# Gated linear attention on one core: attends and value transposes moved to other PSUM banks, and a head's gate work moved beside its own query strips

## The chip, the cores and the metric

The kernel runs on one core of one Trainium2 chip. The metric is the device time of one execution in microseconds (us). TensorE (PE) multiplies matrices into PSUM, VectorE (DVE) and ScalarE (ACT) work on what it leaves there, SyncE (SP) issues the transfers from HBM, and GpSimd (POOL) has nothing to do.

## The reference

The reference is a decoder trunk of two layers over 528 tokens of width 1024 (16 meta tokens and 512 inputs). Layer 0 is gated linear attention (GLA) with 4 heads, a key width of 256 and a value width of 512 per head. Layer 1 is an attention with forget gates (FoX) with 16 heads. What the change touches is layer 0, cut here to what matters:

```python
def gla_layer(h, norm_g, w_in, w_gate_up, b_gate, head_norm_g, w_out):
    proj = rmsnorm(h, norm_g) @ w_in
    q, k, v, g_low, r = jnp.split(proj, [o1, o2, o3, o4], axis=-1)
    log_a = jax.nn.log_sigmoid((g_low @ w_gate_up + b_gate)) / GLA_GATE_NORMALIZER
    q = q.reshape(B, L, GLA_HEADS, GLA_HEAD_K) * (GLA_HEAD_K ** -0.5)
    ...
    o = gla_chunked(q, k, v, log_a)       # S_t = diag(a_t) S_{t-1} + k_t^T v_t, o_t = q_t S_t
    o = rmsnorm(o, head_norm_g).reshape(B, L, D_INNER)
    return h + (o * jax.nn.silu(r)) @ w_out
```

## The kernel before

**Strips.** A strip is a projection of the normalised input onto 128 output columns: `strip(job, x1)` (L1146) runs 8 k-tiles, and for each k-tile three products (high by high, high by low, low by high part) over two halves of 264 tokens, 48 matmuls in all. Its weights come as one 512 KB transfer into `raw`; ACT copies them to `w_hi` (L348) and DVE makes the rest `w_lo` (L684). Both do that in `split`, and `ahead(name)` splits the chunk that lies three strips behind the named one. In `ahead` DVE waits until ACT has made the same chunk's `w_hi`. A head of GLA has 12 strips: two of queries (Q), two of keys (K), four of values (V) and four of the output gate (R).

**Jobs and slots.** PE's work is a list of named jobs. Besides the strips a head has two gate products G (`gate_logits`, L1190: the low-rank gate times its up projection), four value transposes X (`transposed`, L1179) and four attends A (`gla_attend`, L1223, the scores times a 128-column part of the values). The job of each name takes one of two slots of two PSUM banks (banks 0 and 1, or 2 and 3) by the parity of its number in the list (`slot`, L217). `wait_slot` (L254) lets PE write a slot only when the job two places earlier in the list has been read: a Q strip by `q_made`, a K strip by `k_made`, a V strip by `vt_made`, an R strip by `r_made`, a G by `g_abs` and `g_min`, an X by `vlo_made`, an A by `y_made`. The scores (`gla_scores`, L1199) lie in banks 4 to 7, and the sum of squares of the last head's output (`sum_squares`, L1168) in banks 4 and 5.

**The gate chain of a head.** When G{h}0 and G{h}1 are done, ACT takes their absolute value (L387), then the exponential (L389) and the logarithm (L391), each with its own table load, and DVE the minimum with zero (L733), the difference and the running sum `b_` (L739). Then DVE forms four differences of `b_` (`minus_at`), and ACT eleven exponentials of them (`decays`, L396, one table load). DVE multiplies queries and keys with these (`muls_q`, L758, and `muls_k`, L785), and only then can the scores of that head start.

**The order.** Every engine's order is written out by hand. In a head h PE runs: Q0, the sum of squares of head h-1, Q1, K0, K1, V0, R0, X0, V1, scores, R1, A0, X1, V2, then the gate products of head h+1, A1, X2, V3, R2, A2, X3, R3, A3. The gates and decays of head h+1 thus run on ACT and DVE during head h; those of head 0 run in front, during the first strips. `gla_value` (L422) copies a V strip into the one buffer `gvt`, from which X transposes it. `gla_out` (L845) makes `y` of an attend, after ACT has squared the attend (`gla_square`, L454). `head_norm` (L854) is a reciprocal and two multiplications of head h-1's `y`, once ACT's `root` (L360) has read the sum of squares. On DVE `gla_gate` (R strip to `gsr`) of R1 is followed by `ahead("V{h}2")` and `gla_out(h, 0)`.

After the four heads come the output projection (W0 to W7), then the 16 heads of FoX, which use the two slots by the same parity.

The lines that say which jobs exist and where they go:

```python
def slot(job):
    return 2 * (JOB[job] % 2)
...
b = JOBS[JOB[job] - 2]      # wait_slot: whose readers must be done
```

Of the kernel before, what the change touches and what calls it, by code (L numbers as in the profile page):

```python
# [11 lines left out]
P = 128  # L12
# [62 lines left out]
def gla_strips(h):  # L75
    return [f"Q{h}0", f"Q{h}1", f"K{h}0", f"K{h}1", f"V{h}0", f"R{h}0", f"V{h}1", f"R{h}1", f"V{h}2", f"V{h}3", f"R{h}2", f"R{h}3"]
# [18 lines left out]
JOB = {j: n for n, j in enumerate(JOBS)}  # L95

# [15 lines left out]
def program(nc, xT, consts, vecs, w_low, w_up, w_all, w_f, out):  # L112
    with ExitStack() as c:
# [88 lines left out]
        fkf = acc  # L202
        fsr, fvt = sq[:, 0, 0:SEQ], sq[:, 1, :]
# [13 lines left out]
        def slot(job):  # L217
            return 2 * (JOB[job] % 2)

# [34 lines left out]
        def wait_slot(pe, job):  # L254

            if JOB[job] < 2:
                return
            b = JOBS[JOB[job] - 2]
# [82 lines left out]
        def _(act):  # L341
# [39 lines left out]
            def gates(h):  # L381
                for t in range(CT):
                    done(act, f"G{h}{t}")
                    if h:
                        act.wait_ge(mul_made, (h - 1) * len(MULS) + MULS.index("qj0") + 1)
                    col = B_GATE + h * CT + t
                    nc.scalar.activation(two(s1[:, t, :]), halves(slot(f"G{h}{t}")), ACT.Abs, bias=vec[:, col:col + 1]).then_inc(g_abs, 1)  # L387
# [34 lines left out]
            def gla_value(h, v):  # L422
                done(act, f"V{h}{v}")
                if 4 * h + v:
                    before = f"X{h}{v - 1}" if v else f"X{h - 1}3"
                    done(act, before)
                nc.scalar.activation(two(gvt[:]), halves(slot(f"V{h}{v}")), ACT.Copy).then_inc(vt_made, 1)
# [46 lines left out]
            ahead("Q00")  # L474
            ahead("Q01")
            gates(0)
            ahead("K00")
            decays(0)
            for h in range(GLA_HEADS):
                if h:  # L480
# [12 lines left out]
                gla_gate(h, 0)  # L493
# [4 lines left out]
                gla_scores_hi(h)  # L498
                gla_gate(h, 1)
                ahead(f"V{h}2")  # L500
                gla_square(h, 0)
                gla_values_hi(h, 1)
                gla_value(h, 2)
                if h + 1 < GLA_HEADS:
                    gates(h + 1)
                ahead(f"V{h}3")
                gla_square(h, 1)
                gla_values_hi(h, 2)
                if h + 1 < GLA_HEADS:
                    decays(h + 1)  # L510
                gla_value(h, 3)
                ahead(f"R{h}2")
                gla_gate(h, 2)
                ahead(f"R{h}3")
                gla_square(h, 2)
                gla_values_hi(h, 3)
                gla_gate(h, 3)
                if h + 1 == GLA_HEADS:
                    y_high(0)
                gla_square(h, 3)  # L520
# [158 lines left out]
        def _(dve):  # L679
# [43 lines left out]
            dve.wait_ge(rtok_done, 1)  # L723
            nc.vector.tensor_copy(rtok[:, 0:NBLK], bank(6, 0, NBLK * 32).rearrange("p (b n) -> p b n", n=32)[:, :, 0]).then_inc(rtok_made, 1)
            nc.vector.tensor_copy(rtok[0:META, NBLK:NBLK + 1], bank(6, 128, 129, 0, META)).then_inc(rtok_made, 1)

            def gates(h):
                for t in range(CT):
                    dve.wait_ge(g_abs, 2 * h + t + 1)
                    if h:  # L730
                        dve.wait_ge(exp_made, h * len(EXPS))
                    col = B_GATE + h * CT + t
                    nc.vector.tensor_scalar(two(s2[:, t, :]), halves(slot(f"G{h}{t}")), vec[:, col:col + 1], 0.0, ALU.add, ALU.min).then_inc(g_min, 1)  # L733
# [132 lines left out]
            ahead("Q00")  # L866
            gla_query(0, 0)
            ahead("Q01")
            gla_query(0, 1)
            dve.wait_ge(cst_loaded, 16)  # L870
            gates(0)
            ahead("K00")
            decays(0)
            gla_key(0, 0)
            for h in range(GLA_HEADS):
                if h:
                    ahead(f"Q{h}0")
                    gla_query(h, 0)
                    head_norm(h - 1)
                    ahead(f"Q{h}1")  # L880
# [12 lines left out]
                ahead(f"R{h}1")  # L893
                gla_mask(h)
                gla_scores_lo(h)
                gla_gate(h, 1)
                ahead(f"V{h}2")
                gla_out(h, 0)
                gla_values_lo(h, 1)
                if h + 1 < GLA_HEADS:  # L900
                    gates(h + 1)
                ahead(f"V{h}3")
                gla_out(h, 1)
                gla_values_lo(h, 2)
                if h + 1 < GLA_HEADS:
                    decays(h + 1)
                ahead(f"R{h}2")
                gla_gate(h, 2)
                ahead(f"R{h}3")
                gla_out(h, 2)  # L910
                gla_values_lo(h, 3)
                gla_gate(h, 3)
# [212 lines left out]
        def _(pe):  # L1125
# [64 lines left out]
            def gate_logits(h):  # L1190
                for t in range(CT):
                    job = f"G{h}{t}"
                    wait_slot(pe, job)
                    c0 = h * GLA_DK + t * P
                    for n in range(2):
                        i = nc.tensor.matmul(halves(slot(job))[:, n, :], up[:, c0:c0 + P], glow[:, n * HALF:(n + 1) * HALF], start=True, stop=True)
                    i.then_inc(job_done, 1)

            def gla_scores(h):  # L1199
                pe.wait_ge(mul_made, (h + 1) * len(MULS))  # L1200
                pe.wait_ge(rstd_made, h + 1)
                if h == 0:
                    pe.wait_ge(rtok_made, 2)
# [46 lines left out]
            pe.wait_ge(rstd_made, 1)  # L1250
            rstd_by_token()
            pe.wait_ge(glow_made, 1)
            pe.wait_ge(up_loaded, 32)
            gate_logits(0)
            for h in range(GLA_HEADS):
                if h:
                    strip(f"Q{h}0", x1)
                    pe.wait_ge(hacc_made, 3 * h)
# [3 lines left out]
                for s in (f"K{h}0", f"K{h}1", f"V{h}0", f"R{h}0"):  # L1262
                    strip(s, x1)
                pe.wait_ge(vt_made, 4 * h + 1)
                transposed(f"X{h}0", gvt)
# [7 lines left out]
                if h + 1 < GLA_HEADS:  # L1273
                    gate_logits(h + 1)
                gla_attend(h, 1)
                pe.wait_ge(vt_made, 4 * h + 3)
                transposed(f"X{h}2", gvt)
                strip(f"V{h}3", x1)
                strip(f"R{h}2", x1)
                gla_attend(h, 2)  # L1280
                pe.wait_ge(vt_made, 4 * h + 4)
                transposed(f"X{h}3", gvt)
                strip(f"R{h}3", x1)
                gla_attend(h, 3)

# [195 lines left out]
```

## Time and profile before

| | us |
|---|---|
| median of 3 runs | 1192.83 (1192.6 to 1192.99) |
| the profiled execution's own time | 1195.57 |
| its span | 1193.8 |
| PE busy | 1107.8 (93%) |
| DVE busy | 612.2 (51%) |
| ACT busy | 496.3 (42%) |
| mean granted clock of PE | 0.965 of full |

The profiled execution is 2.7 us above the median, and its span leaves 1.8 us of its own time outside. PE is the engine to read: what counts is where it waits, and which chain on ACT and DVE ends the wait. The four GLA heads take the first 451 us, the output projection and FoX the rest.

### The profile page before, as it was taken

The page shows a single profiled execution, that of the slowest core. Times are in us where ns is not written, and L with a number is a line of the kernel's source. Part 1 is how long each engine was busy: PE and PEld are TensorE (multiplying, and loading weights), DVE is VectorE, ACT ScalarE, POOL GpSimd, SP SyncE. Part 2 cuts the span into 40 slices and gives each one's busy share as a digit, 9 for nine tenths or more (in the row PEclk, how much of TensorE's full clock was granted, in tenths as well). Part 3 has the DMA queues.
Part 4 walks back from the last instruction along what each step waited for, and adds up shares of the span by engine and source line. Part 5 has one row for each costly group of instructions (what it writes and reads, how often), then busy time and mean ns, then how long its engine had stood idle before and what let it go on. Part 6 is the DMA issues. An engine that isn't in the chain of part 4 may idle for free.

```text
span 1193.8 us, 18411 instructions
## 1 busy us (share of the span) xinstructions
PE 1107.8 (93%) x7716; PEld 1011.7 (85%) x7716; DVE 612.2 (51%) x1032; ACT 496.3 (42%) x869; POOL 0.2 (0%) x4
## 2 busy tenths in 40 slices
PE   6897999799799999999799999999999999998995
PEld 5786998799799899998688888888888888886883
DVE  5664473556457437535445554455455555564233
ACT  5624523723452325424434444444444444454221
POOL 0000000000000000000000000000000000000000
PEclk9898999899999999999899999999999999998997
DMA  6111121112112111222111222112211212211211
GB/s 224 53 54 36 54 89 54 42 65 89 37 54 80 63 54 57 103 89 71 54 66 59 71 71 71 57 68 72 71 57 68 71 55 70 72 56 51 92 50 70
DMA packets 23762, 81.77 MB, mean 68 GB/s; under 512 B 2784, under 2 KB 3040, under 8 KB 23680
## 3 DMA queue, kind: packets, MB, share of 16 engines
q1 hardware_dynamic: 23680, 80.59, 19.4%
q8 instruction: 61, 1.00, 0.3%
q14 instruction: 21, 0.17, 0.0%
HBM read 78.49 MB, written 2.10 MB: 68 GB/s over the span
## 4 chain that ended last, share of the span: by engine, by line
PE 83%; DVE 9%; ACT 4%; issue 3%; DMA 0%; DVEq 0%; ACTq 0%; SPq 0%
PE psum L1138 68%; PE psum L1378 3%; PE psum L1364 2%; PE psum L1207 2%; DVE w_lo L684 2%; ACT w_hi L348 1%; DVE y L691 1%; PE psum L1347 1%; PE psum L1361 1%; PE psum L1349 1%; PE psum L1350 1%; PE psum L1348 1%; DVE y L845 1%; DVE gsr L691 1%; DVE y_lo L691 1%
## 5 line engine op out<-in xcount | busy, mean ns | idle before, releaser
L684 DVE TENSOR_TENSOR w_lo<-raw,w_hi 128x1024 fp32r<-128x1024 f32 x144 | 174.9, 1220 | 81.9 <-ACT w_hi L348 81.7
L1138 PE MATMUL psum<-xh,w_hi 128*128 128x264 f32 x768 | 165.1, 297 | 35.6 <-DVE y L845 27.9
L348 ACT ACTIVATE w_hi<-raw 128x1024 fp32r<-128x1024 f32 x144 | 149.9, 1048 | 100.0 <-PE psum L1138 100.0
L1138 PE MATMUL psum<-xl,w_hi 128*128 128x264 f32 x768 | 161.0, 292 | 0.0
L1138 PE MATMUL psum<-xh,w_lo 128*128 128x264 f32 x768 | 160.0, 291 | 0.0
L1138 PEld LDWEIGHTS psum<-xh,w_hi 128*128 128x128 f32 x768 | 124.3, 197 | 40.8 <-DVE w_lo L684 29.1
L1138 PEld LDWEIGHTS psum<-xl,w_hi 128*128 128x128 f32 x768 | 124.3, 196 | 0.0
L1138 PEld LDWEIGHTS psum<-xh,w_lo 128*128 128x128 f32 x768 | 124.2, 196 | 0.0
L1138 PE MATMUL psum<-zh,w_hi 128*128 128x264 f32 x512 | 106.2, 289 | 5.9 <-DVE y L691 3.2
L1138 PE MATMUL psum<-zl,w_hi 128*128 128x264 f32 x512 | 104.4, 286 | 0.0
L1138 PE MATMUL psum<-zh,w_lo 128*128 128x264 f32 x512 | 104.1, 285 | 0.0
L1138 PE MATMUL psum<-x2h,w_hi 128*128 128x512 f32 x256 | 103.3, 404 | 0.0
L1138 PE MATMUL psum<-y_lo,w_hi 128*128 128x264 f32 (+1 forms) x384 | 102.1, 320 | 0.0
L1138 PE MATMUL psum<-x2h,w_lo 128*128 128x512 f32 x256 | 101.8, 398 | 0.0
L1138 PE MATMUL psum<-x2l,w_hi 128*128 128x512 f32 x256 | 101.0, 395 | 0.0
L1138 PEld LDWEIGHTS psum<-zh,w_hi 128*128 128x128 f32 x512 | 80.8, 190 | 10.5 <-issue 9.0
L1138 PEld LDWEIGHTS psum<-zl,w_hi 128*128 128x128 f32 x512 | 79.9, 189 | 0.0
L1138 PEld LDWEIGHTS psum<-zh,w_lo 128*128 128x128 f32 x512 | 79.7, 189 | 0.0
L1003 DVE TENSOR_REDUCE top<-psum 128x1 f32<-128x144 f32 (+1 forms) x64 | 30.8, 504 | 78.3 <-PE psum L1351 78.3
L1138 PEld LDWEIGHTS psum<-y_lo,w_hi 128*128 128x128 f32 x384 | 63.7, 188 | 5.8
L1138 PEld LDWEIGHTS psum<-x2h,w_lo 128*128 128x128 f32 x256 | 48.1, 188 | 11.3
L1138 PEld LDWEIGHTS psum<-x2l,w_hi 128*128 128x128 f32 x256 | 48.3, 188 | 10.8
(239 smaller groups left out, 1896.8 us busy)
## 6 DMA issues: line engine op xcount, KB each, us to landing
raw<-w_all SPq DMA_DIRECT2D x144, 512.0 KB, 3.2
hT<-xT SPq DMA_DIRECT2D x8, 264.0 KB, 5.4
outT<-hT SPq DMA_DIRECT2D x8, 256.0 KB, 2.3
cst<-consts SPq DMA_DIRECT2D x1, 528.0 KB, 6.9
y<-w_up_ SPq DMA_DIRECT2D x2, 64.0 KB, 8.1
low_raw<-w_low SPq DMA_DIRECT2D x1, 64.0 KB, 2.1
f_raw<-w_f SPq DMA_DIRECT2D x1, 64.0 KB, 8.2
vec<-vecs SPq DMA_DIRECT2D x1, 22.5 KB, 1.6
```

The costliest lines, as they stand in the source:

```text
L348: nc.scalar.activation(w_hi[:, n % HI_RING, :], raw[:, n % LO_RING, :], ACT.Copy).then_inc(hi_made, 1)
L684: nc.vector.tensor_tensor(w_lo[:, n % LO_RING, :], raw[:, n % LO_RING, :], w_hi[:, n % HI_RING, :].bitcast(F32), ALU.subtract).then_inc(lo ...
L691: nc.vector.tensor_tensor(out, a, b, op).then_inc(made, 1)
L845: nc.vector.scalar_tensor_tensor(y[:, n, :], joined(slot(f"A{h}{v}")), vec[:, G_HEAD + v:G_HEAD + v + 1], gsr[:, v % 2, :], op0=ALU.mult, ...
L1003: nc.vector.tensor_reduce(top[:, b:b + 1], scores(b), op=ALU.max, axis=AX.XY if b == NBLK - 1 else AX.X, negate=True).then_inc(max_made, 1)
L1138: i = nc.tensor.matmul(o, w[a][:, k % KT, :], x[b][:, k, c0:c1], start=k == first and a == b == 0, stop=k == last and a == 1)
L1207: i = nc.tensor.matmul(out, lhs[:, t], rhs[:, t], start=t == 0, stop=t == CT - 1)
L1347: nc.tensor.matmul(o, fq_hi[:, cols], fk_hi[:, k0:k1], start=True, stop=False)
L1348: nc.tensor.matmul(o, fq_hi[:, cols], fk_lo[:, k0:k1], start=False, stop=False)
L1349: nc.tensor.matmul(o, fq_lo[:, cols], fk_hi[:, k0:k1], start=False, stop=False)
L1364: i = nc.tensor.transpose(bank(bk, c0, c0 + BLK), pr[b][:, BLK * j:BLK * j + BLK], ident)
L1378: i = nc.tensor.matmul(bank(slot(job), PT_Q0[j], SEQ), vs[a][0:rows, j, :], ps[b][0:rows, AF_AT[j]:AF_AT[j] + w], start=j == 0 and a == b ...
```

## The change

- The place of a job is now a table, `PLACE`. Attends (and G01) go to banks 4 and 5, value transposes and the other gate products to banks 6 and 7, and the strips (with the jobs of the later stages) alternate on the two old slots. `wait_slot` waits for the readers of the job that was last in the same place (`BEFORE`).
- `gvt` becomes two buffers, the second of them a row of `y`.
- The gate products of head h+1 leave the middle of head h: G{h+1}0 comes at the end of head h, and G{h+1}1 behind Q{h+1}0. The absolute values, the exponential, the logarithm, the running sum and the decays of a head now run in that head, beside its Q and K strips: between `ahead` of Q0 and `ahead` of K1.
- In those parts the key strip K0 is read (`gla_key(h, 0)`) in the middle of DVE's decays, and K1 behind them and behind `ahead("K{h}1")`.
- V3 and R2 change places, each A and X comes behind the next strip, the scores follow R1, and the scores now also wait for X0's readers. `rstd_by_token` moves from ahead of head 0's gate products to between K00 and K01.

```diff
 def gla_jobs(h):
-    gate = [f"G{h + 1}0", f"G{h + 1}1"] if h + 1 < GLA_HEADS else []
-    first = ["G00", "G01"] if h == 0 else []
-    return ([f"Q{h}0", f"Q{h}1"] + first + [f"K{h}0", f"K{h}1", f"V{h}0", f"R{h}0", f"X{h}0", f"V{h}1", f"R{h}1", f"A{h}0", f"X{h}1",
-            f"V{h}2"] + gate + [f"A{h}1", f"X{h}2", f"V{h}3", f"R{h}2", f"A{h}2", f"X{h}3", f"R{h}3", f"A{h}3"])
+    first = ["Q00", "Q01", "G00", "G01"] if h == 0 else [f"Q{h}0", f"G{h}1", f"Q{h}1"]
+    return (first + [f"K{h}0", f"K{h}1", f"V{h}0", f"R{h}0", f"X{h}0", f"V{h}1", f"R{h}1", f"V{h}2", f"A{h}0", f"X{h}1", f"R{h}2",
+                     f"A{h}1", f"X{h}2", f"V{h}3", f"A{h}2", f"X{h}3", f"R{h}3", f"A{h}3"] + ([f"G{h + 1}0"] if h + 1 < GLA_HEADS else []))
...
+PLACE, BEFORE = {}, {}
+_slots = 0
+for _job in JOBS:
+    if _job[0] == "A" or _job == "G01":
+        PLACE[_job] = 4
+    elif _job[0] in "XG":
+        PLACE[_job] = 6
+    else:
+        PLACE[_job] = 2 * (_slots % 2)
+        _slots += 1
+    _same = [j for j in PLACE if PLACE[j] == PLACE[_job]]
+    BEFORE[_job] = _same[-2] if len(_same) > 1 else None
...
@@ ACT, one head (h > 0) @@
+                    gate_abs(h, 0)
                     ahead(f"Q{h}0")
+                    gate_abs(h, 1)
                     root(f"h{h - 1}", GLA_DV, T)
+                    gate_log(h)
+                    ahead(f"Q{h}1")
...
                     ahead(f"K{h}0")
+                decays(h)
                 ahead(f"K{h}1")
                 ahead(f"V{h}0")
                 gla_value(h, 0)
...
@@ DVE, one head (h > 0) @@
+                    gate_min(h, 0)
                     ahead(f"Q{h}0")
                     gla_query(h, 0)
+                    gate_min(h, 1)
+                    ahead(f"Q{h}1")
                     head_norm(h - 1)
-                    ahead(f"Q{h}1")
                     gla_query(h, 1)
-                    ahead(f"K{h}0")
-                    gla_key(h, 0)
+                gate_sums(h)
+                ahead(f"K{h}0")
+                decays(h)
                 ahead(f"K{h}1")
+                gla_key(h, 1)
                 muls_q(h)
-                gla_key(h, 1)
                 ahead(f"V{h}0")
                 muls_k(h)
                 ahead(f"R{h}0")
                 gla_gate(h, 0)
...
@@ DVE decays @@
                 minus_at(s1, 32, 15)
                 minus_at(s2, 64, 31)
+                gla_key(h, 0)
                 exped(h, "kd")
                 minus_at(s1, 128, 63)
...
@@ PE, one head @@
                 if h:
                     strip(f"Q{h}0", x1)
+                    gate_logits(h, 1)
                     pe.wait_ge(hacc_made, 3 * h)
                     pe.wait_ge(glo_made, 5 * h)
                     sum_squares(f"h{h - 1}")
                     strip(f"Q{h}1", x1)
...
                 strip(f"V{h}1", x1)
+                strip(f"R{h}1", x1)
                 gla_scores(h)
-                strip(f"R{h}1", x1)
+                strip(f"V{h}2", x1)
                 gla_attend(h, 0)
-                pe.wait_ge(vt_made, 4 * h + 2)
-                transposed(f"X{h}1", gvt)
-                strip(f"V{h}2", x1)
-                if h + 1 < GLA_HEADS:
-                    gate_logits(h + 1)
+                gla_transposed(h, 1)
+                strip(f"R{h}2", x1)
                 gla_attend(h, 1)
...
                 strip(f"R{h}3", x1)
                 gla_attend(h, 3)
+                if h + 1 < GLA_HEADS:
+                    gate_logits(h + 1, 0)
```

## Rows read from the trace of the kernel before

**Rows 1.** The page: PE's busy time and granted clock over the whole span

```profile
PE 1107.8 (93%) x7716; PEld 1011.7 (85%) x7716; DVE 612.2 (51%) x1032; ACT 496.3 (42%) x869; POOL 0.2 (0%) x4
...
PEclk9898999899999999999899999999999999998997
```

**Rows 2.** Windows by head; stretch, its length, busy times, PE clock, DMA

```profile
18.32:144.33 126.01, 109.42 (x826) 103.72 (x826) 65.57 (x99) 58.43 (x98) 0.00 (x0) 0.89 0.17 58
...
250.13:355.96 105.83, 96.62 (x813) 93.22 (x813) 56.77 (x89) 44.26 (x75) 0.00 (x0) 0.95 0.17 60
355.96:451.14 95.18, 91.23 (x804) 88.59 (x804) 47.65 (x81) 30.41 (x55) 0.00 (x0) 1.00 0.19 68
```

**Rows 3.** The chain that ended last, head 2; start, length, piece

```profile
257.04 29.21 PE psum L1138 x240
...
293.22 6.33 PE psum L1207 x125
...
316.10 1.99 PE psum L1196 x8
...
329.29 13.61 PE psum L1138 x96
...
347.34 6.08 PE psum L1138 x48
...
355.96 6.03 PE psum L1138 x48
361.98 0.89 PE psum L1170 x4
```

**Rows 4.** Waits of PE in head 2 (257 to 363 us): total, times, longest

```profile
PE psum L1138 <- DVE y L845: 8.1, 3, 5.5
```

**Rows 5.** Timeline of ACT around head 2's gate chain and the next root

```profile
318.83 1.28 ACT L389 ACT_TABLE_LOAD   x1
320.13 1.08 ACT L389 ACTIVATE s<-s 128x1056 f32<-128x1056 f32 x1
...
332.25 1.28 ACT L400 ACT_TABLE_LOAD   x1 [5.95 <-DVE s L691]
...
340.14 0.59 ACT L427 ACTIVATE gvt<-psum 128x528 f32<-128x528 f32 x1
340.63 1.05 ACT L348 ACTIVATE w_hi<-raw 128x1024 fp32r<-128x1024 f32 x1
...
362.91 0.70 ACT L360 ACTIVATE sq<-psum,eps 128x528 f32<-128x528 f32 x1 [4.06 <-PE psum L1170]
```

**Rows 6.** Timeline of DVE in the same head

```profile
257.81 3.45 DVE L696 RECIPROCAL acc<-sq 128x528 f32<-128x528 f32 x1 [0.92 <-ACT sq L360]
...
263.65 1.22 DVE L684 TENSOR_TENSOR w_lo<-raw,w_hi 128x1024 fp32r<-128x1024 f32 x1
264.79 0.70 DVE L800 SCALAR_TENSOR_TENSOR q<-psum,rstd 128x528 f32<-128x528 f32 x1
...
271.06 1.22 DVE L691 TENSOR_TENSOR qd<-qd,q 128x1024 f32<-128x1024 f32 x1
...
281.46 0.18 DVE L691 TENSOR_TENSOR km<-km,k 128x32 f32<-128x32 f32 x1
...
323.65 1.26 DVE L691 TENSOR_TENSOR s<-s 128x1056 f32<-128x1056 f32 x1 [4.03 <-ACT s L391]
324.94 2.41 DVE L739 TENSOR_TENSOR_SCAN b<-cst,s 128x528 f32<-128x528 f32 x2
...
330.97 2.34 DVE L691 TENSOR_TENSOR s<-b 128x1024 f32<-128x1024 f32 x2
```

**Rows 7.** Timeline of PE: four of the five transposes of a value strip

```profile
286.19 0.60 PE L1184 MATMUL psum<-cst,gvt 128*128 128x128 f32 x4
```

**Rows 8.** The chain that ended last, head 0 and the end of head 3

```profile
32.71 0.70 DVE y L691
...
65.52 7.62 PE psum L1138 x48
...
442.51 6.09 PE psum L1138 x48
```

More of the change, by code:

```diff
@@ L75, in gla_strips @@
 def gla_strips(h):
[L76 removed]
+    return [f"Q{h}0", f"Q{h}1", f"K{h}0", f"K{h}1", f"V{h}0", f"R{h}0", f"V{h}1", f"R{h}1", f"V{h}2", f"R{h}2", f"V{h}3", f"R{h}3"]
 def gla_jobs(h):
[L80 to L83 removed]
+    first = ["Q00", "Q01", "G00", "G01"] if h == 0 else [f"Q{h}0", f"G{h}1", f"Q{h}1"]
+    return (first + [f"K{h}0", f"K{h}1", f"V{h}0", f"R{h}0", f"X{h}0", f"V{h}1", f"R{h}1", f"V{h}2", f"A{h}0", f"X{h}1", f"R{h}2",
+                     f"A{h}1", f"X{h}2", f"V{h}3", f"A{h}2", f"X{h}3", f"R{h}3", f"A{h}3"] + ([f"G{h + 1}0"] if h + 1 < GLA_HEADS else []))
 def fox_step(h):
@@ L202, in program @@
         fkf = acc
+        gvt2 = (gvt[:], y[:, YT - 1, :])
         fsr, fvt = sq[:, 0, 0:SEQ], sq[:, 1, :]
@@ L217, in slot @@
         def slot(job):
-            return 2 * (JOB[job] % 2)
+            return PLACE[job]
         def joined(b):
@@ L254, in wait_slot @@
         def wait_slot(pe, job):
-            if JOB[job] < 2:
+            b = BEFORE[job]
+            if b is None:
                 return
-            b = JOBS[JOB[job] - 2]
             kind = b[0]
@@ L379, in _, with gate_abs, gate_log @@
             root("x", D_MODEL, T)
[L381 to L387, printed above, removed]
+            def gate_abs(h, t):
+                done(act, f"G{h}{t}")
+                if h:
+                    act.wait_ge(mul_made, (h - 1) * len(MULS) + MULS.index("qj0") + 1)
+                col = B_GATE + h * CT + t
+                nc.scalar.activation(two(s1[:, t, :]), halves(slot(f"G{h}{t}")), ACT.Abs, bias=vec[:, col:col + 1]).then_inc(g_abs, 1)
+            def gate_log(h):
                 act.wait_ge(g_abs, 2 * h + 2)
@@ L423, in gla_value @@
                 done(act, f"V{h}{v}")
[L424 to L427, printed above, removed]
+                if 4 * h + v >= 2:
+                    done(act, f"X{h}{v - 2}" if v >= 2 else f"X{h - 1}{v + 2}")
+                nc.scalar.activation(two(gvt2[v % 2]), halves(slot(f"V{h}{v}")), ACT.Copy).then_inc(vt_made, 1)
             def gla_values_hi(h, v):
@@ L472, in y_high @@
                     nc.scalar.activation(y_hi[:, i, :], y[:, i, :], ACT.Copy).then_inc(yhi_made, 1)
[L474 to L478, printed above, removed]
-            for h in range(GLA_HEADS):
-                if h:
+            for h in range(GLA_HEADS):
+                if h == 0:
+                    ahead("Q00")
+                    ahead("Q01")
+                    gate_abs(0, 0)
+                    gate_abs(0, 1)
+                    gate_log(0)
+                    ahead("K00")
+                else:
+                    gate_abs(h, 0)
                     ahead(f"Q{h}0")
+                    gate_abs(h, 1)
                     root(f"h{h - 1}", GLA_DV, T)
+                    gate_log(h)
+                    ahead(f"Q{h}1")
                     if h == 1:
@@ L492, in _ @@
                 ahead(f"R{h}0")
-                gla_gate(h, 0)
                 gla_values_hi(h, 0)
@@ L497, in _ @@
                 ahead(f"R{h}1")
-                gla_scores_hi(h)
+                gla_gate(h, 0)
                 gla_gate(h, 1)
                 ahead(f"V{h}2")
+                gla_scores_hi(h)
+                gla_value(h, 2)
                 gla_square(h, 0)
                 gla_values_hi(h, 1)
-                gla_value(h, 2)
-                if h + 1 < GLA_HEADS:
-                    gates(h + 1)
-                ahead(f"V{h}3")
+                ahead(f"R{h}2")
+                gla_gate(h, 2)
                 gla_square(h, 1)
                 gla_values_hi(h, 2)
-                if h + 1 < GLA_HEADS:
-                    decays(h + 1)
+                ahead(f"V{h}3")
                 gla_value(h, 3)
-                ahead(f"R{h}2")
-                gla_gate(h, 2)
-                ahead(f"R{h}3")
                 gla_square(h, 2)
                 gla_values_hi(h, 3)
+                ahead(f"R{h}3")
                 gla_gate(h, 3)
@@ L722, in _, with gate_min, gate_sums @@
             tt(glow, glow, rstd[0:48, :], ALU.mult, glow_made)
[L723 to L733, printed above, removed]
+            def gate_min(h, t):
+                dve.wait_ge(g_abs, 2 * h + t + 1)
+                if h:
+                    dve.wait_ge(exp_made, h * len(EXPS))
+                col = B_GATE + h * CT + t
+                nc.vector.tensor_scalar(two(s2[:, t, :]), halves(slot(f"G{h}{t}")), vec[:, col:col + 1], 0.0, ALU.add, ALU.min).then_inc(g_min, 1)
+            def gate_sums(h):
                 dve.wait_ge(g_ln, h + 1)
@@ L864, in y_low @@
                     tt(y_lo[:, i, :], y[:, i, :], y_hi[:, i, :].bitcast(F32), ALU.subtract, ylo_made)
[L866 to L874, printed above, removed]
-            for h in range(GLA_HEADS):
-                if h:
+            for h in range(GLA_HEADS):
+                if h == 0:
+                    ahead("Q00")
+                    gla_query(0, 0)
+                    ahead("Q01")
+                    gla_query(0, 1)
+                    gate_min(0, 0)
+                    gate_min(0, 1)
+                    dve.wait_ge(rtok_done, 1)
+                    nc.vector.tensor_copy(rtok[:, 0:NBLK], bank(6, 0, NBLK * 32).rearrange("p (b n) -> p b n", n=32)[:, :, 0]).then_inc(rtok_made, 1)
+                    nc.vector.tensor_copy(rtok[0:META, NBLK:NBLK + 1], bank(6, 128, 129, 0, META)).then_inc(rtok_made, 1)
+                    dve.wait_ge(cst_loaded, 16)
+                else:
+                    gate_min(h, 0)
                     ahead(f"Q{h}0")
                     gla_query(h, 0)
+                    gate_min(h, 1)
+                    ahead(f"Q{h}1")
                     head_norm(h - 1)
-                    ahead(f"Q{h}1")
                     gla_query(h, 1)
-                    ahead(f"K{h}0")
-                    gla_key(h, 0)
+                gate_sums(h)
+                ahead(f"K{h}0")
+                decays(h)
                 ahead(f"K{h}1")
+                gla_key(h, 1)
                 muls_q(h)
-                gla_key(h, 1)
                 ahead(f"V{h}0")
@@ L893, in _ @@
                 ahead(f"R{h}1")
+                gla_gate(h, 1)
+                ahead(f"V{h}2")
                 gla_mask(h)
                 gla_scores_lo(h)
-                gla_gate(h, 1)
-                ahead(f"V{h}2")
                 gla_out(h, 0)
                 gla_values_lo(h, 1)
-                if h + 1 < GLA_HEADS:
-                    gates(h + 1)
-                ahead(f"V{h}3")
+                ahead(f"R{h}2")
+                gla_gate(h, 2)
                 gla_out(h, 1)
                 gla_values_lo(h, 2)
[L905 to L909, printed above, removed]
+                ahead(f"V{h}3")
                 gla_out(h, 2)
                 gla_values_lo(h, 3)
+                ahead(f"R{h}3")
                 gla_gate(h, 3)
@@ L1188, in _, with gate_logits @@
             x1 = (xh[:], xl[:])
[L1190 to L1197, printed above, removed]
+            def gate_logits(h, t):
+                job = f"G{h}{t}"
+                wait_slot(pe, job)
+                c0 = h * GLA_DK + t * P
+                for n in range(2):
+                    i = nc.tensor.matmul(halves(slot(job))[:, n, :], up[:, c0:c0 + P], glow[:, n * HALF:(n + 1) * HALF], start=True, stop=True)
+                i.then_inc(job_done, 1)
             def gla_scores(h):
@@ L1201, in gla_scores @@
                 pe.wait_ge(rstd_made, h + 1)
-                if h == 0:
-                    pe.wait_ge(rtok_made, 2)
+                pe.wait_ge(vlo_made, 4 * h + 1)
                 def mm(out, lhs, rhs):
@@ L1249, in _, with gla_transposed @@
             strip("Q01", x1)
-            pe.wait_ge(rstd_made, 1)
-            rstd_by_token()
             pe.wait_ge(glow_made, 1)
             pe.wait_ge(up_loaded, 32)
-            gate_logits(0)
+            gate_logits(0, 0)
+            gate_logits(0, 1)
+            def gla_transposed(h, v):
+                pe.wait_ge(vt_made, 4 * h + v + 1)
+                transposed(f"X{h}{v}", gvt2[v % 2])
             for h in range(GLA_HEADS):
@@ L1261, in _ @@
                     strip(f"Q{h}1", x1)
[L1262 to L1265, printed above, removed]
+                strip(f"K{h}0", x1)
+                if h == 0:
+                    pe.wait_ge(g_min, 1)
+                    pe.wait_ge(rstd_made, 1)
+                    rstd_by_token()
+                strip(f"K{h}1", x1)
+                strip(f"V{h}0", x1)
+                strip(f"R{h}0", x1)
+                if h == 0:
+                    pe.wait_ge(rtok_made, 2)
+                gla_transposed(h, 0)
                 strip(f"V{h}1", x1)
+                strip(f"R{h}1", x1)
                 gla_scores(h)
-                strip(f"R{h}1", x1)
+                strip(f"V{h}2", x1)
                 gla_attend(h, 0)
-                pe.wait_ge(vt_made, 4 * h + 2)
-                transposed(f"X{h}1", gvt)
-                strip(f"V{h}2", x1)
-                if h + 1 < GLA_HEADS:
-                    gate_logits(h + 1)
+                gla_transposed(h, 1)
+                strip(f"R{h}2", x1)
                 gla_attend(h, 1)
-                pe.wait_ge(vt_made, 4 * h + 3)
-                transposed(f"X{h}2", gvt)
+                gla_transposed(h, 2)
                 strip(f"V{h}3", x1)
-                strip(f"R{h}2", x1)
                 gla_attend(h, 2)
-                pe.wait_ge(vt_made, 4 * h + 4)
-                transposed(f"X{h}3", gvt)
+                gla_transposed(h, 3)
                 strip(f"R{h}3", x1)
                 gla_attend(h, 3)
+                if h + 1 < GLA_HEADS:
+                    gate_logits(h + 1, 0)
             ys = (y_hi[:], y_lo[:])
```

## The prediction

> **What bounds the kernel now.** I read the page first: PE is busy 93% of the span and its clock dips only in places, DVE and ACT are half idle [rows 1]. So time can only come from PE's waits and from the low clock behind them. The windows by head say where: head 0 takes 126.0 us from its first strip, heads 1 and 2 take 105.8 each (one of the two stands), and head 3, which makes no gates for a next head, 95.2 [rows 2]. The chain of waits of head 2 gives the pieces [rows 3]: five strips in a row take 29.21 us, 5.84 each; a strip with something else ahead of it takes 6.05; the scores 6.33; a gate product 1.0 (two in 1.99); the sum of squares 0.89; an attend 2.54 (from the end of the strip at 347.34 to 355.96). A value transpose is 0.75 (four of its five in 0.60 [rows 7]).
>
> In that chain PE stands still from 318.1, the end of the two gate products, to 329.3, but for one attend and one transpose. The gate products sit in the slots, so A1 waits for their readers, and V3 waits for `y` of A1, which on DVE is queued behind the gates' chain: ACT's load, exponential, load and logarithm end at 323.65, 4.82 us after the first load began [rows 5, 6], then the difference and the sums. That is the 5.5 us wait; two shorter waits on `y` (2.6 together, 1.3 each) stand behind the other attends [rows 4]. After the long gap PE starts at its lower level: two strips take 13.61 instead of 11.9 [rows 3].
>
> **The change part by part.** I put t = 0 at the start of a head's Q0 strip and walk all queues, heads 1 to 3 first.
>
> *Strips alone on the slots, A and X elsewhere, G out of the middle.* V2, R2, V3 and R3 wait only for the last strip but one in their slot, whose reader is done. Each attend has a strip between it and the next, 6 us for the square and the `y` (0.6 and 0.8 each), so A costs no wait; X needs `vlo_made` of the X before, also a strip away. The second `gvt` frees the V copy. So from the end of R0 I count no wait: X0 0.75, V1 and R1 11.9, scores 6.33, V2 6.05; three times attend, transpose and strip, 9.34 each; A3 and the next G 3.54. Sum 56.6 us. What hides the splitting of the scores now is V2, as R1 did.
>
> *The gate chain beside the head's own Q strips.* It is moved, not removed, and here it sits on the path. PE: Q0 to 6.03, G{h}1 to 7.03, sum of squares to 7.9. ACT: absolute value 0.70 (a row of this size [rows 5]) to 7.75, load for the root 1.28 to 9.05, root 0.70 to 9.75, then load, exponential, load, logarithm 4.82 to 14.6, and only then `ahead` of Q1, the `w_hi` of V0, 1.05 to 15.6. DVE stands in its own `ahead` of Q1 until that: `w_lo` 1.14 to 16.75 (pitch from 263.65 to 264.79), reciprocal and multiplications of `head_norm` 5.84 (257.81 to 263.65) to 22.6, the Q1 query 0.70 to 23.3 [rows 6]. K1 has Q1's slot: it starts at 23.4, where PE was there at 19.8. **First wait, 3.6 us.**
> Then DVE: difference and sums 3.7 to 26.9, `w_lo` of R0 1.14 to 28.05, first decay difference 1.17 to 29.2, second 30.4, key K0 31.1. V0 has K0's slot: 31.2, against 29.5 for K1's end (31.0 if the clock fell, then no gap). ACT from 29.2: load and eleven exponentials 7.89 (332.25 to 340.14) to 37.1, `w_hi` of V1 1.05 to 38.15 [rows 5]; DVE is held in `ahead` of K1 again: `w_lo` 39.3, key K1 0.70 to 40.0. R0 has K1's slot and starts at 40.15, V0 having ended at 37.3. **Last wait, 2.9 us**, and this one sets the head: a slow K1 or V0 is swallowed by it.
>
> *The clock.* No row shows a gap of 3 us ahead of a strip in heads 1 to 3, so I bound it. Below: nothing, 6.05. Above: R0 at half speed throughout, 5.84 more. The nearest row is the strip at 65.52, which came after a 1.9 us wait and took 7.62, 1.55 above 6.05 [rows 8]; I take 1.55. R0 ends at 47.75.
> Head 1 or 2: 47.75 + 56.6 = 104.35 against 105.8, a gain of 1.5, twice 3.0. Head 3, to the end of A3: 103.35 against 95.2, a **loss of 8.15**: it had its gate chain made in head 2 and now pays for it itself.
>
> *Head 0.* The gate factor is ready at 33.4 [rows 8]. G00 and G01 have free banks and run 33.55 to 35.55, K00 to 41.6, the transposes of the root (at most 0.75, as X) to 42.35, K01 to 48.4. ACT's logarithm ends at 36.3 + 4.82 = 41.1, but DVE now waits for those transposes: sums from 42.6 to 46.3, `w_lo` 47.45, first difference 48.6, K00 read at 50.5, V00 at 50.6 after a gap of 2.2. ACT: exponentials 6.6 without the load, which can run ahead here, to 55.2, `w_hi` 56.3, `w_lo` 57.4, key 58.1. R00 starts at 58.25, against 65.52, and a slow V00 ends just then, so R00 runs at full clock to 64.3. Behind it 56.6 us free of waits: the Q strip of head 1 starts at 120.9 instead of 144.3 (18.32 + 126.01 [rows 2]), **23.4 earlier**: head 1's chain has left this head, with its 8 us of standing still in an 11 us stretch, its slow strips, one of the G and the waits on `y`.
>
> *Behind the four heads* nothing changes but a shift. The rest (removed order in `gvt`, V3 and R2 swapped, the weights' transfers in the new order, never waited for here) I cost at nothing; they are hidden by strips of 6 us, and the DMA share is 0.17 to 0.19 [rows 2].
>
> Sum: -23.4 - 3.0 + 8.15 = -18.3 us. The profiled execution took 1195.57, so its like would be 1177.3; the median of the runs is 2.7 lower, and 1192.83 - 18.3 = **1174.5**.
>
> **A rule weighed against a row.** The load before the exponential takes 1.28 us, and the exponential starts 0.02 us behind its end [rows 5]: nothing else stands between. The Trainium skill ("ScalarE: Activation LUTs", What ACT_TABLE_LOAD costs) gives 1283 ns for the load, with which the row agrees, and adds a drain of about 1380 ns, 2.66 us per switch. By that page's figure the 14 loads on my path (four in each of heads 1 to 3, two in head 0) would take another 19.3 us, an estimate from the page, and nothing would be gained. The sum stays with the rows.
>
> **The rivals.**
> 1. *The clock stays high in R0.* For it: waits of 1.3 us in head 2 cost no speed. Against: the strip at 65.52 [rows 8]. Heads 1 and 2 are then 3.05 faster each, head 3 loses 6.6: -23.4 - 6.1 + 6.6 = -22.9, 1169.9.
> 2. *R1 becomes late.* It has R0's slot, whose reader is queued on DVE behind the q and k products and `w_lo` of V2: from 39.9 another 9.95 (271.06 to 281.64, less the key [rows 6]), 1.14 and 0.70, so 51.7; PE is there at 54.5, or 53.0 at high clock. For it: the margin is small. If those operations took half as long again, 5.9 us, R1 would lose 3.1 in four heads: 12.4, 1186.9.
> 3. *The waits on `y` stay.* Attends have one pair of banks, so A1, A2, A3 wait for `y` as strips do now. Twelve such waits at 1.3 us [rows 4] are 15.6: 1190.1. Against: a strip of 6 us lies between.
> 4. *All waits hide*: the K and V strips cover the chain. Heads 1 to 3 then take 10.6 less each, 1142.7. Against: key K1 comes after 40 us of serial work, and PE without waits would want R0 at 7.9 + 4 x 5.9 = 31.5.
> 5. *A switch of tables costs twice its row.* Something of the length of a load, 1.28, is hidden in the old places and not on this path: 14 x 1.28 = 17.9, 1192.4, no change. Against: the 0.02 us. This is the case in which the page's drain would bite.
> 6. *Slower: the clock, once down, stays down.* Place: R0, X0 and V1 of heads 1 to 3, after three gaps in a row. Each strip at half speed costs up to 5.84. It decides when more than (18.3 + 2.4) / 5.84 = 3.5 strips go that way, just over one further strip a head; with two more strips a head it is 35 us, 1209.6. Against: in head 2 two strips after an 11 us stretch lost 1.7 together [rows 3].
>
> **How the numbers follow.** Forecast 0.64, rivals 1 to 6: 0.13, 0.07, 0.08, 0.03, 0.02, 0.03. 0.2% is 2.4 us, about what a measurement of this kernel tells from no change. Faster takes the forecast, 1, 2, 4 and most of 3: 0.93; same a part of 3 and 5: 0.04; slower 0.03. The range takes the forecast with its clock bounds and rival 1 on the low side, and half of rival 2 on the high side: 1168.5 to 1182.5.
>
> **What would show it.** Window of heads 1 to 3: three gaps of PE, ahead of K1, V0 and R0, the first ended by the query on DVE, the last two by the keys, and none behind R0 but handoffs. `w_lo` of V0 on DVE should start at about 15.6, waiting for ACT, and R0 at 40. Head 0's successor starts at 121. A last head of about 103 us shows the loss. Wrong would be: waits on `y` ahead of A1 to A3, on `gsr` ahead of R1, R0 before 38 or after 43, or a slow strip in the second half of a head.

## The result, and the profile after

| | before | after |
|---|---|---|
| median, us | 1192.91 (1192.6 to 1196.08, 4 runs) | 1166.89 (1166.66 to 1171.12, 4 runs) |
| ratio | | 0.9783 (0.9767 to 0.9798) |
| profiled execution's own time | 1195.57 | 1171.12 |
| its span | 1193.8 | 1169.3 |

The change is 26.0 us faster by the medians, 24.45 by the two profiled executions. The profiled execution of the changed kernel is the longest of its four; the other three took 1166.66 to 1167.11. The forecast was 18.3 us and 1174.5, with a range from 1168.5: the direction and the order of the waits held, and the time came out 1.6 us below the range.

The page after, PE's share:

```profile
PE 1101.1 (94%) x7716; PEld 1008.0 (86%) x7716; DVE 610.7 (52%) x1032; ACT 492.2 (42%) x866; POOL 0.2 (0%) x4
```

The windows after, one for each head, from its first strip (the last one to the end of A3); the columns are those of [rows 2]:

```profile
18.36:120.48 102.12, 99.44 (x822) 95.93 (x822) 55.73 (x91) 44.06 (x76) 0.00 (x0) 0.97 0.20 68
...
223.54:326.60 103.06, 96.40 (x813) 93.14 (x813) 56.44 (x90) 42.97 (x74) 0.00 (x0) 0.97 0.19 62
326.60:428.60 102.00, 95.23 (x808) 92.31 (x808) 56.68 (x90) 43.50 (x76) 0.00 (x0) 0.97 0.19 62
```

Against [rows 2] head 0 went from 126.0 to 102.1, heads 1 and 2 from 105.8 to 103.06, and head 3 from 95.2 to 102.0. Most of the gain is in head 0, which made two gate chains before (its own and head 1's) and makes one now, and the last head, which made none and makes one now, gives 6.8 us of it back.

The chain that ended last, head 2 after (start, length, piece):

```profile
223.54 6.04 PE psum L1153 x48
...
231.42 1.28 ACT L373
232.72 0.70 ACT sq L373
...
238.12 1.05 ACT w_hi L361
...
240.34 3.46 DVE acc L711
...
246.25 0.62 DVE q L814
...
262.90 0.71 DVE k L706
...
263.75 7.60 PE psum L1153 x48
...
271.90 11.69 PE psum L1153 x96
```

From the first strip it is PE for 7 us, then 33 us in which ACT and DVE hand each other the gate chain, and R0 at 263.75, 40.21 us into the head. It takes 7.60 instead of 6.05, part of it at the low clock, and behind it the chain does not leave PE again until it is past the next head's Q0 strip and second gate product. The windows over R0 and over a part of it give the granted clock (the last number but two):

```profile
263.75:271.35 7.60, 7.60 (x50) 7.58 (x51) 7.53 (x17) 0.37 (x1) 0.00 (x0) 0.78 0.00 0
265.75:267.75 2.00, 2.00 (x11) 2.00 (x11) 1.97 (x7) 0.00 (x0) 0.00 (x0) 0.50 0.00 0
```

0.50 is the lower of the two levels, 1.2 of 2.4 GHz. PE's waits in that head:

```profile
PE psum L1153 <- DVE q L814: 3.6, 1, 3.6
PE psum L1153 <- DVE k L706: 3.1, 1, 3.1
```

The waits on `y` of [rows 4] are gone. The two that are left are the ones ahead of K1 and R0; V0 has none, since K1 ran slowly too (granted clock 0.78 from 247.01 to 254.70).

**Outside the heads.** By the start of W1's strips the two chains are 22.55 us apart (479.03 before, 456.48 after). The other 1.9 us of the profiled pair come behind that, in work which the change does not touch; for instance the last sum of squares, 0.95 us of them, is the same two matmuls at another clock level. The chain at the end of the kernel before:

```profile
1179.62 2.09 PE psum L1407 x2
```

and of the changed kernel:

```profile
1156.11 1.14 PE psum L1429 x2
```

### The profile page after: what moved, and what is told of

The parts are those of the page before. It is cut to its first block, busy times and chain, and to the rows that moved or that the text cites. A ratio compares the mean times of both kernels' runs of the same rounds, so it can differ in the third digit from the quotient of the medians.

```text
span 1169.3 us, 18409 instructions
## 1 busy us (share of the span) xinstructions
PE 1101.1 (94%) x7716; PEld 1008.0 (86%) x7716; DVE 610.7 (52%) x1032; ACT 492.2 (42%) x866; POOL 0.2 (0%) x4
## 4 chain that ended last, share of the span: by engine, by line
PE 81%; DVE 9%; ACT 6%; issue 3%; DMA 0%; DVEq 0%; SPq 0%; ACTq 0%
PE psum L1153 63%; PE psum L1400 3%; PE psum L1386 2%; PE psum L1220 2%; PE psum L1250 2%; DVE y L706 1%; DVE s L706 1%; PE psum L1369 1%; ACT w_hi L361 1%; DVE w_lo L699 1%; PE psum L1383 1%; DVE acc L711 1%; PE psum L1371 1%; PE psum L1372 1%; PE psum L1370 1%
## 5 line engine op out<-in xcount | busy, mean ns | idle before, releaser
L1153 PE MATMUL psum<-xh,w_hi 128*128 128x264 f32 x768 | 166.3, 299 | 23.4 <-DVE k L706 11.4
L1153 PE MATMUL psum<-y_lo,w_hi 128*128 128x264 f32 (+1 forms) x384 | 102.1, 320 | 0.0
```

What stands on the lines that cost most here:

```text
L1153: i = nc.tensor.matmul(o, w[a][:, k % KT, :], x[b][:, k, c0:c1], start=k == first and a == b == 0, stop=k == last and a == 1)
```

## The experiments

All kernels of this section but e1 start from the changed kernel. The kernel before ran beside each group; its medians were 1194.28 (e1 to e4), 1195.00 (e5, e6) and 1194.17 (e7 to e9), so the ratios are what to compare. The changed kernel has 0.9783 and, once more, 0.9791.

**e1, the places alone.** The kernel before with

```diff
-    return 2 * (JOB[job] % 2)
+    return PLACE[job]          # A, G00, G01: 4; X and other G: 6; the rest 0 and 2 in turn
-    b = JOBS[JOB[job] - 2]
+    b = BEFORE[job]
```

(cut to what matters; the scores also wait for X0's readers, as in the changed kernel).

> The kernel before with the new places alone: attends in banks 4 and 5, transposes and gate products in 6 and 7 (G00 and G01 in 4), one gvt, the old order on every engine, gates of head h+1 still in the middle of head h. Theory P (the places carry the gain; moving the gates only trades one chain on the path for another): the waits of 1.3, 5.5 and 1.3 us on y ahead of strips go, one of about 3.5 us ahead of X3 (its copy of V3 stands behind ACT's decays) takes their place; about 7 us gained in each of three heads, 2.6 in head 3: about 1168. Rival M (the place of the gates carries it: y of A1 is still queued behind them and A2 waits for it): 1183 or more.

Measured: 1182.46, ratio 0.9893 (0.9868 to 0.9917), 12.8 us by the ratio: between the two, nearer to the rival. A middle head takes 101.7 us, from the Q strip at 245.42 to the one at 347.12, a gain of 4.1 and not 7. PE's waits in that stretch:

```profile
PE psum L1194 <- ACT gvt L439: 3.6, 1, 3.6
PE psum L1208 <- DVE s L745: 1.7, 1, 1.7
```

The 3.6 us ahead of X3 are the ones expected. The second was missed: both gate products now have one place, so the second waits for the readers of the first, and behind it the clock falls. The nine matmuls of A0 and of A1 at the same line in the chain:

```profile
301.17 1.21 PE psum L1248 x9
...
314.89 2.14 PE psum L1248 x9
```

So the places alone are worth half of the change. A middle head is even shorter here than in the changed kernel (103.06), but head 0 is not: it takes 122.9 us (from 18.53 to 141.45), where the changed kernel takes 102.1.

**e2, the order alone.**

```diff
-    if _job[0] == "A" or _job == "G01":
-        PLACE[_job] = 4
-    elif _job[0] in "XG":
-        PLACE[_job] = 6
-    else:
-        PLACE[_job] = 2 * (_slots % 2)
-        _slots += 1
+    PLACE[_job] = 2 * (_slots % 2)
+    _slots += 1
```

> The changed kernel with one thing undone: all jobs share the two old slots by parity again. Theory P: R2, V3, R3 and Q of the next head wait again for y of the attend two jobs before, 1.2 us each, 4 in each head, some 19 us: about 1186. Rival M (order is what counts): 1167 to 1170.

Measured: 1219.72, ratio 1.021 (1.0194 to 1.0225): 25 us slower than the kernel before, worse than the theory had it. PE's waits in one head (258 to 362 us):

```profile
PE psum L1148 <- DVE gsr L701: 5.0, 1, 5.0
PE psum L1148 <- DVE k L701: 4.6, 2, 3.1
PE psum L1148 <- DVE y L854: 3.6, 4, 1.0
PE psum L1148 <- DVE q L809: 3.6, 1, 3.6
```

The four waits on `y` are there, 0.9 each. What the theory left out is the first line: with X0 counted among the jobs on the slots, V1 lies two places behind R0 and waits 5 us for R0's reader, which DVE does only behind all products of the head. The order needs the places.

**e8, attends back on the strips' slots.**

```diff
-    if _job[0] == "A" or _job == "G01":
+    if _job == "G01":
```

> The changed kernel with the attends put back on the two slots of the strips; transposes and gate products stay in banks 6 and 7. A head then has 16 jobs on the slots, and the job two places ahead of each is always one whose reader has had a strip's time. Theory (it is enough that transposes and gate products leave the slots): no new wait, the time of the changed kernel within 1 us, 1166 to 1168. Rival (the attends' own banks are needed): a wait on y of 1 us in front of three strips a head, 12 us more.

Measured: 1169.99, ratio 0.9796 (0.9779 to 0.9814), beside the changed kernel's 1168.83 and 0.9791 on the same chip: no difference beyond the noise, and no wait on the `y` of an attend among PE's waits. Of the new places those of the transposes and gate products are the ones that pay, once each attend has a strip ahead and behind.

**e5, the first wait taken away.**

```diff
+                    gla_query(h, 1)
                     ahead(f"Q{h}1")
                     head_norm(h - 1)
-                    gla_query(h, 1)
```

> The changed kernel, and DVE reads strip Q1 ahead of the split of V0's weights and of the head norm instead of behind them, so that PE's first wait, 3.6 us ahead of K1, goes. Theory (the last wait, ahead of R0, sets the head): only the 0.6 us of the query leave the chain to R0, three times: 1.9 us, about 1165. Rival (each wait counts): 3.6 us three times and the low clock behind it: about 1156 or less.

Measured: 1166.19, ratio 0.9759 (0.9745 to 0.9774), 3 to 4 us below the changed kernel. The wait on the query is gone from PE's list, and the waits on the keys have grown from 11.4 us in all to

```profile
PE psum L1153 <- DVE k L706: 19.6, 8, 4.7
```

A wait that is not the last one of its head is worth little: nearer to the theory's 1.9 than to the rival's 11. The trace shows why it is still more than 1.9: heads 1 and 2 are 100.9 us long, 2.1 less than 103.06, of which 0.6 is the query and 1.5 is R0, which takes 6.08 here in each of the three heads instead of 7.60.

**e3, the last wait taken away.**

```diff
-                ahead(f"K{h}1")
                 gla_key(h, 1)
+                ahead(f"K{h}1")
```

> The changed kernel, and DVE reads strip K1 ahead of its split of V1's weights instead of behind it. Theory (a wait that goes brings the next one up): R0 starts when V0 ends, 2.9 us earlier and at full clock, but then R1 comes at 49.8 us into the head and its slot's reader is done only at 51.8, so about 2.4 us in each of heads 1 to 3 and 0.9 in head 0 are left: about 1159. Rival: the whole wait and the low clock behind it are earned, 4.45 us three times: 1153.

Measured: 1166.05, ratio 0.9767 (0.9751 to 0.9784), 2 to 3 us and not the theory's 8. The chain in the same head:

```profile
269.33 1.14 DVE w_lo L699
270.46 0.63 DVE gsr L706
271.23 7.59 PE psum L1153 x48
```

R1 starts 51.2 us into the head (first strip at 219.99), as the theory had it (51.8). The next wait came up, behind DVE's products and the split of V2, 1.9 us long, and with it the low clock moved from R0 to R1: 7.59 us. This head is 101.84 long, from 219.99 to the next at 321.83, 1.2 less than in the changed kernel. The theory forgot that last term. It is paid in this head only: in heads 1 and 3 R1 stands behind 0.9 and 1.3 us and takes 6.08, and head 1 is 100.34 long. Another part of the shortfall is likely in the base of the theory: it took its terms from the profiled execution, in which R0 is slow in all three heads, and its 1159 from the median (e7 below).

**e4, ACT's split ahead of the root.**

```diff
                     gate_abs(h, 1)
+                    ahead(f"Q{h}1")
                     root(f"h{h - 1}", GLA_DV, T)
                     gate_log(h)
-                    ahead(f"Q{h}1")
```

> The changed kernel, and ACT makes the high part of V0's weights ahead of the root and the logarithm instead of behind them, one move in ACT's queue. Theory (DVE's queue stands in that split, so the head norm's 5.8 us start 6 us late): R0 starts 5.85 us earlier in heads 1 to 3, 17.5 in all: about 1149.4. Rival (the logarithm sets DVE's sums anyway): 1 us a head, about 1164.

Measured: 1148.94, ratio 0.9617 (0.9601 to 0.9633), some 20 us below the changed kernel by the ratio. The chain of one head:

```profile
217.25 6.04 PE psum L1153 x48
...
225.02 1.05 ACT w_hi L361
...
228.11 3.46 DVE acc L711
...
250.69 0.71 DVE k L706
...
251.53 6.08 PE psum L1153 x48
```

R0 starts at 251.53, 34.3 us into the head as worked out, and at full clock. The second is why this head lost 7.45 us (95.61 instead of 103.06) and not 5.85. In head 1 of the same trace R0 starts as early, behind the same wait of 2.7 us, but takes 7.48, and the head is 97.00 long. In the changed kernel DVE stands 7.0 us in front of `w_lo` of V0, and the head norm, the query, the sums and the keys all stand behind it:

```profile
DVE w_lo L699 <- ACT w_hi L361: 13.5, 4, 7.0
```

(the row is DVE's in head 2 of the changed kernel; 7.0 is its longest).

**e9, all three reads first, in the wrong place.** The edits of e4 and e3, and

```diff
-                    head_norm(h - 1)
                     gla_query(h, 1)
+                    head_norm(h - 1)
```

> The changed kernel with ACT's high part of V0 ahead of the root, query Q1 read ahead of the whole head norm and key K1 as soon as the decays are formed; unlike the kernel with all moves, reciprocal and multiplications stay together, behind the query. Theory (DVE stands still for Q1 from 10 to 14 us into the head with the head norm behind it, so the chain is 3 us later than with the split alone): V0 waits 2.8 us, R1 1 to 2 us, heads of 97 us against 95.6 with the split alone: about 1153. Rival (three waits named, three waits removed): 1141 or less.

Measured: 1156.74, ratio 0.9685 (0.9670 to 0.9699): 8 us slower than with the split alone. The chain of one head:

```profile
217.74 6.04 PE psum L1153 x48
...
232.46 3.46 DVE acc L711
...
265.52 0.63 DVE gsr L706
266.29 6.08 PE psum L1153 x48
```

DVE waits for strip Q1 until 231.8 and only then begins the reciprocal, 3.9 us later into the head than in e4 (14.7 against 10.9). V0 waits 2.65 us and R1, which starts at 48.55, 0.34 here and up to 1.85 in head 3; heads 1 and 2 take 97.6 us. The waits are about those expected, and the time is 3 to 4 us above the theory's 1153.

**e6, all moves.** ACT as in e4, key K1 as in e3, and on DVE:

```diff
                     ahead(f"Q{h}1")
-                    head_norm(h - 1)
+                    head_root(h - 1)           # the reciprocal alone
                     gla_query(h, 1)
...
-                ahead(f"R{h}0")
                 gla_gate(h, 0)
+                ahead(f"R{h}0")
                 gla_values_lo(h, 0)
+                if h:
+                    head_scale(h - 1)          # the two multiplications
```

with the copies of `rtok` behind `gate_sums(0)`.

> The changed kernel with DVE's and ACT's queues put in the order in which PE wants the results: ACT's high part of V0 ahead of the root; DVE's reciprocal, then query Q1, the sums and decays, key K1 as soon as the decays are formed, R0's reader ahead of the split of V2, and the two multiplications of the head norm behind R0's reader; the copies of rtok behind the sums of head 0. Nothing is left out. Theory: PE finds K1, V0, R0 and R1 free and heads 1 to 3 take 92.5 us instead of 103.1; with 1 to 2 us in head 0 about 1133 to 1135. Rival (a wait of 1 to 3 us ahead of R1 on DVE's chain of products comes up, as it did when the key alone was read first): 1140 or more.

Measured: 1138.15 (1136.58 to 1138.81), ratio 0.9524 (0.9507 to 0.9541) to the kernel before, 56.9 us; that is 31 to 32 us below the changed kernel by the ratios. The window of head 2 (head 1's has the same length and the same busy time) and its first part in the chain:

```profile
209.24:301.90 92.66, 92.66 (x813) 89.94 (x813) 56.40 (x90) 43.10 (x74) 0.00 (x0) 1.00 0.21 69
```

```profile
209.24 6.04 PE psum L1162 x48
215.28 1.08 PE psum L1219 x4
216.37 1.09 PE psum L1194 x4
217.45 29.20 PE psum L1162 x240
```

A head is 92.66 us and PE is busy for 92.66 of them at full clock; it has no wait left in heads 1 to 3. This version beats both kernels, with the same instructions.

**e7, the changed kernel again, nothing edited.**

> The changed kernel once more, nothing edited, beside the others on one chip. Theory (of the 26.0 us of the first comparison 22.5 are the waits and pieces of the four heads, the rest is where the clock falls, which differs from run to run in one and the same kernel): the runs spread over 1 to 4 us with their mean clock, and the ratio to the kernel before comes out between 0.978 and 0.981, 23 to 26 us. Rival (the later stages are really faster): the same 26.0 us within 0.5.

Measured: 1168.83 (1166.61 to 1171.32, 5 runs), ratio 0.9791 (0.9774 to 0.9808), 25 us. One kernel on one chip spread over 4.7 us, and the kernel before over 4.6 (1192.78 to 1197.38, 9 runs). The mean clocks of single runs (0.976 to 0.978, and 0.960 to 0.968) do not order their times. But the profiled execution of this group took 1166.61, 4.5 us less than the profiled one of the first comparison, and the two chains can be laid side by side. The Q0 strips of heads 1, 2 and 3 and the R0 strips behind them:

```profile
118.57 6.04 PE psum L1153 x48
158.79 6.08 PE psum L1153 x48
220.12 6.04 PE psum L1153 x48
260.34 7.53 PE psum L1153 x48
323.10 6.04 PE psum L1153 x48
363.32 6.08 PE psum L1153 x48
```

R0 starts 40.22 us into each head, as in the first trace, but it is slow in head 2 alone, where the first trace has 7.60 or 7.61 in all three. In head 0 K00 takes 6.05 here and 7.55 there, and the head is 1.9 us shorter. In heads 1 and 3 more of the loss fell on K1, where the wait ahead of R0 swallows it (granted clock 0.64 from 142.04 to 149.60, where K1 of head 2 in the first trace has 0.78). W1's strips start at 451.46 instead of 456.48. Those 5.0 us are 1.9 in head 0 and 1.5 each in heads 1 and 3: one kernel, the same order and the same queues, and only the places where the clock fell differ. The runs without a trace may differ in the same way; that is not shown.

## Why the prediction was right, and where it was wrong

**The waits came as forecast, almost row by row.** In the first trace R0 was forecast at 40.15 us into a head and came at 40.21; K1 at 23.4 and came at 23.47; its wait 3.6 and 3.6; the wait ahead of R0 2.9 and 3.1; a slow R0 7.6 and 7.60. There was no wait behind R0. The third gap named as a sign, ahead of V0, was absent: K1 was slow and filled it, as the forecast allowed. The first matmuls of K1 and R0 in the timeline of PE, head 2 after, with the wait ahead of each in brackets:

```profile
247.01 0.48 PE L1153 MATMUL psum<-xh,w_hi 128*128 128x264 f32 x2 [3.58 <-DVE q L814]
...
263.75 0.48 PE L1153 MATMUL psum<-xh,w_hi 128*128 128x264 f32 x2 [3.07 <-DVE k L706]
```

Head 3 pays for its own gate chain, and head 0 brings the gain: forecast 23.4 earlier, measured 23.85 (144.33 to 120.48).

**The step that failed is a term's size: "from the end of R0 ... Sum 56.6 us".** It measures 55.25 (R0 ends at 168.29, the next head starts at 223.54), in each of four heads (the last one without the next G). I took 6.05 us for each strip behind other work and 0.75 for a transpose. The strips that stand near 6.05 in the rows began behind a wait, behind the scores or behind an attend. One that is queued behind a transpose takes 5.84 like one in a row of strips, and the transpose before it 0.65 in the chain (0.21 and 0.44):

```profile
289.91 6.02 PE psum L1153 x48
...
298.45 0.21 PE psum L1197
298.66 0.44 PE psum L1199 x4
299.10 5.84 PE psum L1153 x48
```

Attend, transpose and strip are 9.01 here (289.91 + 6.02 to 299.10 + 5.84) instead of 9.34. Four times 1.35 is 5.4, by which the forecast was too long. Head 0 takes 0.9 back, since R00 started at 59.16 and not at 58.25: K00 ran at the low clock (7.55), so the transposes of the root behind it, and with them DVE's sums, came 1 us later (43.61, not 42.6). That makes 22.8 us for the four heads against the 22.55 measured.

**The second term: the clock in R0.** I took 1.55 us of lost clock in each of heads 1 to 3, one value for every run. The first trace has it in all three. The trace of e7, the same kernel, has 1.45 in head 2 and nothing in heads 1 and 3, and its K00 is at full clock as well; that makes 5.0 us between two executions. The forecast is of the median, and three of the first four runs took 1166.66 to 1167.11, like e7's profiled 1166.61; it is likely, but without their traces not shown, that the clock fell in them as in e7.

**What the range left out.** With the sum put right the four heads give 22.55 us and a median of 1170.3, inside the range. Behind the heads I forecast a pure shift; the profiled pair gained 1.9 us more there, and the medians lie another 1.5 us further apart than the pair. With e7 the change is worth 25 to 26 us. The range was built from the bounds of single terms around a sum that was 4 us too long; a spread of some 4 us between runs of one kernel (e7) should have been in it.

**The rivals.** Rival 1 (full clock in R0) fell in the first trace, by the 7.60, and held in two of the three heads in e7's; its 1169.9 is nearer to the result than the forecast. Rival 2 (R1 late) did not happen, but it was the next wait in line: e3 and e9 brought it up, 1.9 us at most in each. Rival 3 (the waits on `y` stay) fell, and e8 shows that it would not even have come true with fewer banks. Rival 4 (all waits hide) fell for this kernel, and e6 is that case. Rival 5 fell: the chain's loads cost what the row said, 1.28 us with the next activation 0.02 behind (231.42 + 1.28, then 232.72), and R0 came at 40.21. The Trainium skill ("ScalarE: Activation LUTs", What ACT_TABLE_LOAD costs) adds a drain of about 1380 ns to every switch; by that page the four switches ahead of R0 would have put it 5.5 us later, an estimate from the page, which this trace does not bear out. Rival 6 fell: the clock was low in a part of K1 and of R0 and full again (1.00 from 271.35 to 277).

**What the parts are worth.** The places alone 12.8 us, the order alone minus 25, both 25 to 26: they don't add. No run moves the gate chain alone, so its share is argued from e1 and the changed kernel, which also differ in the order of the A, X, V3 and R2 jobs and in the second `gvt`. By that comparison it is no gain for the middle heads (103.06 against 101.7 in e1). It took work out of head 0 (102.1 against 122.9) that [rows 2] had there, and put the chain where one move in ACT's queue (e4) and then a better order on DVE (e6) could hide it altogether.

## What to carry to other kernels

When several waits of one chain show up in a stage, find the last one and follow the chain back through both engines' queues: taking away an earlier wait (e5) or the last alone (e3) gave 2 to 4 us, and moving one 1 us copy ahead of a 7 us block on the engine that feeds the chain (e4) gave 20. Read a result as soon as it is there, but not ahead of work that could start sooner (e9): in an in-order queue a read that waits is itself a block. The order of the waits and the start of R0 were the same in two traces of one kernel, and the strips that the clock slowed were not: a term for the clock wants a lower and an upper value, and a range as wide as the spread between runs. When a sum has many equal terms, take each one's duration from a row with the same neighbour ahead of it, queued or waited for.

## What the runs showed of the hardware

The strip of 48 matmuls takes, at full clock, 5.84 to 5.86 us behind a strip, transposes or the sum of squares, when it is queued behind them; 6.02 to 6.04 behind the scores, an attend or a gate product; and 6.07 to 6.09 behind a wait. The kernel's very first strip stands outside this (7.4 to 8.2 in the traces).

A strip that the clock slows is not slow throughout: R0 of the changed kernel had a granted clock of 0.78 over its 7.60 us and 0.50 in the middle of it.

The length of a gap of PE does not by itself set the loss behind it. In e4 R0 stands behind the same wait of 2.7 us in all three heads, the only one in each, and took 7.48, 6.08 and 6.08. The first of them, beside the second in the chain of e4 above (251.53, 6.08):

```profile
154.53 7.48 PE psum L1153 x48
```

In e5 V0 stands behind the same wait of 4.73 us in three heads and took 7.4, 8.1 and 8.7 (to the end that R0's start less its wait gives). R1 took 7.59 behind 1.86 us in e3 and 6.07 behind 1.85 us in e9. No run here varied one gap by itself, so what decides stays open. Of the two prices that I had for R0, nothing and 1.55 us, both occur, in one kernel and in one trace.
